# Attention outputs of two heads in the column halves of TensorE's array, and probabilities divided ahead of their transposes

## The reference

```python
def one_block(args):
    blk, qn, qr = args
    s = (jnp.einsum("bqhd,bkhd->bhqk", qn, k_nope) + jnp.einsum("bqhr,bkr->bhqk", qr, k_rope)) * scale
    q_chunk = (blk * Q_BLOCK + jnp.arange(Q_BLOCK)) // CHUNK
    mask = k_chunk[None, :] <= q_chunk[:, None]
    s = jnp.where(mask[None, None], s, -jnp.inf)
    p = jax.nn.softmax(s, axis=-1).astype(v.dtype)
    return jnp.einsum("bhqk,bkhd->bqhd", p, v)
...
return o.reshape(B, S, MLA_HEADS * V_DIM) @ w_o
```

## Time and profile before

| | us |
|---|---|
| median of three runs | 1141.02 |
| the profiled execution | 1142.03 |
| span of its instructions | 1140.2 |
| TensorE busy | 1116.9 (98%) |
| VectorE busy | 874.8 (77%) |
| ScalarE busy | 753.8 (66%) |
| layer 0's head loop, up to the first part of the next slab | 126.6 to 189.2 |
| layer 1's | 552.6 to 615.2 |

### The profile page before, as it was taken

The page is one execution under the profiler, slowest core; times in us unless marked ns, Lnnn a source line. Parts: engine busy times, 40 slices in busy tenths (PEclk is TensorE's granted clock), DMA queues, the critical chain, the costliest instruction groups (busy, mean ns, idle before and its releaser), DMA issues.

```text
span 1140.2 us, 15735 instructions
## 1 busy us (share of the span) xinstructions
PE 1116.9 (98%) x5566; PEld 946.3 (83%) x5566; DVE 874.8 (77%) x983; ACT 753.8 (66%) x941; POOL 35.1 (3%) x64
## 2 busy tenths in 40 slices
PE   9999999999999999999999999999999999999996
PEld 8888888888888888888888888887778887888885
DVE  6568677765554456468676779999999899999997
ACT  6555656455344345556656456799987898988785
POOL 3001000000000001001001000000000000000000
PEclk9999999999999999999999999999999999999999
DMA  9745533668555354646534647999999999999993
GB/s 324 275 147 185 173 95 104 209 216 311 185 184 185 110 182 141 217 135 189 167 102 133 197 174 275 389 403 408 415 417 372 377 402 411 396 417 405 413 369 140
DMA packets 120555, 294.96 MB, mean 259 GB/s; under 512 B 9007, under 2 KB 33677, under 8 KB 119965
## 3 DMA queue, kind: packets, MB, share of 16 engines
q1 hardware_dynamic: 119072, 288.23, 69.8%
q0 software_dynamic: 960, 5.28, 1.2%
q10 hardware_dynamic: 444, 0.47, 0.1%
HBM read 292.90 MB, written 1.05 MB: 258 GB/s over the span
## 4 chain that ended last, share of the span: by engine, by line
PE 77%; DVE 17%; issue 2%; ACT 2%; DMA 1%; ACTq 0%; SPq 0%; DVEq 0%
PE bank L1720 21%; PE bank L1722 21%; PE bank L1721 21%; DVE w_lo L1495 11%; DVE w_lo_more L1495 3%; PE bank L2134 2%; PE bank L1936 2%; PE bank L2135 2%; PE bank L1956 2%; PE bank L1764 2%; PE bank L1944 1%; DVE hid_buf L1634 1%; PE bank L2117 1%; DMA raw<-in_moe_w_gate 1%; PE bank L1925 1%
## 5 line engine op out<-in xcount | busy, mean ns | idle before, releaser
L1166 DVE TENSOR_TENSOR w_lo<-raw,w_hi 128x1024 fp32r<-128x1024 f32 (+4 forms) x141 | 240.3, 1709 | 140.5 <-ACT w_hi L725 139.8
L725 ACT ACTIVATE w_hi<-raw 128x1024 fp32r<-128x1024 f32 (+5 forms) x141 | 201.5, 1433 | 149.0 <-PE bank L1722 149.0
L1495 DVE TENSOR_TENSOR w_lo<-raw,w_hi 128x1792 fp32r<-128x1792 f32 (+3 forms) x148 | 286.4, 1964 | 10.4 <-ACT w_hi L945 9.9
L945 ACT ACTIVATE w_hi<-raw 128x1792 fp32r<-128x1792 f32 (+3 forms) x148 | 244.1, 1668 | 44.7 <-PE bank L1722 29.9
L1720 PE MATMUL bank<-w_hi,aT_hi 128*128 128x512 f32 (+1 forms) x592 | 235.1, 397 | 1.1 <-DVE w_lo L1288 0.6
L1722 PE MATMUL bank<-w_hi,aT_lo 128*128 128x512 f32 (+1 forms) x592 | 229.8, 388 | 0.0
L1721 PE MATMUL bank<-w_lo,aT_hi 128*128 128x512 f32 (+1 forms) x592 | 229.3, 387 | 0.0
L1722 PEld LDWEIGHTS bank<-w_hi,aT_lo 128*128 128x128 f32 x592 | 111.1, 188 | 22.7
L1720 PEld LDWEIGHTS bank<-w_hi,aT_hi 128*128 128x128 f32 x592 | 111.3, 188 | 22.4 <-DVE w_lo L1288 1.6
L1721 PEld LDWEIGHTS bank<-w_lo,aT_hi 128*128 128x128 f32 x592 | 111.4, 188 | 20.3
L1495 DVE TENSOR_TENSOR w_lo_more<-raw,w_hi_more 128x1792 fp32r<-128x1792 f32 (+3 forms) x50 | 96.7, 1940 | 4.5 <-ACT w_hi_more L945 4.5
(11 more groups left out here) (326 smaller groups left out, 1803.1 us busy)
## 6 DMA issues: line engine op xcount, KB each, us to landing
raw<-in_moe_w_gate SPq DMA_DIRECT2D x128, 448.0 KB, 6.6
raw<-in_moe_w_up SPq DMA_DIRECT2D x128, 448.0 KB, 6.4
raw<-in_moe_w_down SPq DMA_DIRECT2D x112, 512.0 KB, 6.6
raw<-in_w_in SPq DMA_DIRECT2D x40, 768.0 KB, 4.4
raw<-in_dense_w_gate SPq DMA_DIRECT2D x22, 512.0 KB, 3.9
raw<-in_dense_w_up SPq DMA_DIRECT2D x22, 512.0 KB, 4.7
raw<-in_dense_w_down SPq DMA_DIRECT2D x11, 1024.0 KB, 4.9
raw<-in_w_in SPq DMA_DIRECT2D x20, 512.0 KB, 4.9
```

The costliest lines, as they stand in the source:

```text
L725: act.activation(dst, src, ACT.Copy).then_inc(hi_made[j], 1)
L945: act.activation(split_of(hi_slot, m), raw_of(i, n), ACT.Copy).then_inc(e_hi_made, 1)
L1166: dve.tensor_tensor(dst, src, high, ALU.subtract).then_inc(lo_made[j], 1)
L1495: dve.tensor_tensor(split_of(lo_slot, m), raw_of(i, n), split_of(hi_slot, m).bitcast(F32), ALU.subtract).then_inc(e_lo_made, 1)
```

## The change

PV is turned around: a head's 64 columns of v are stationary, and pT moves, 256 columns for the first 128 keys and 128 columns for the second (only the second query tile sees those). Two heads make a pair: head x of the pair writes partitions 64x to 64x + 63 of one bank, so its weights stand in one half of the array's columns; the four matmuls alternate between the heads. PV of a pair is issued in even slots from 4 to 18. Its output has channels in the partitions, so VectorE copies it as it is into `oT` (one instruction of 256 columns per pair) and the 16 transposes behind the loop go; ScalarE and VectorE split `oT`, which lies in SBUF, in the places where they split the banks before (`attended_hi`, `attended_lo`).

As tokens are then in the columns, the division by the row sums can't follow PV. VectorE multiplies P by the reciprocals in `p_buf`, ahead of its transposes, and TensorE waits for that (`p_scaled`). VectorE waits for its own reciprocal first. pT has two buffers, for even and odd heads; `qT` has moved to make room. The waits on the count of transposes are renumbered by `transposed`, those on PV by `head_pairs`. Cut to its core:

```diff
-        row_inv = (small[:, 26:28], small[:, 32:34])
+        row_inv = small[:, 26:28]
...
-        mask, p_buf, pT, gain = regions(
-            [("mask", [P, 3 * P]), ("p_buf", [P, 3 * P]), ("pT", [P, 3 * P])],
+        mask, p_buf, pT_even, gain = regions(
+            [("mask", [P, 3 * P]), ("p_buf", [P, 3 * P]), ("pT_even", [P, 3 * P])],
             [("gain", [P, D])])
-        rope_k = place("rope_k", [P, 4, NT, RH])
-        k_rope = place("k_rope", [P, NT, ROPE])
+        rope_k, k_rope, qT = regions(
+            [("rope_k", [P, 4, NT, RH]), ("k_rope", [P, NT, ROPE])],
+            [("qT", [P, S])])
...
-        qT, s_buf = mixed[:, 0, NB:NB + S], mixed[:, 1, NB:NB + 3 * P]
+        s_buf = mixed[:, 1, NB:NB + 3 * P]
+        pT = (pT_even[:, :], mixed[:, 0, NB:NB + 3 * P])
+        oT = xs[:, :, :].rearrange("p t (c s) -> p (t c) s", s=S)
...
+
+        def transposed(use, n):
+
+            return 4 * (use - (use + 2) // 4) + n + 1
+
+        def head_pairs(L, pairs):
+
+            return HEADS // 2 * L + pairs
...
-                pool.wait_ge(o_made, HEADS * (L + 1))
+                pool.wait_ge(o_made, head_pairs(L + 1, 0))
...
                 def transposed_p_in(n):
                     act.wait_ge(p_tr, HEADS * L + n - 1)
-                    if n >= 3:
-                        act.wait_ge(o_made, HEADS * L + n - 2)
-                    act.activation(pT[:, :], bank[B_PT][:, 0:3 * P], ACT.Copy).then_inc(p_in, 1)
+                    if n >= 4:
+                        act.wait_ge(o_made, head_pairs(L, n // 2 - 1))
+                    act.activation(pT[n % 2], bank[B_PT][:, 0:3 * P], ACT.Copy).then_inc(p_in, 1)
+
+                def attended_hi(banks):
+                    act.wait_ge(used[2], B + BLK_GATE + 3)
+                    for n in banks:
+                        act.wait_ge(o_in, head_pairs(L, 2 * n + 2))
+                        act.activation(aT_hi[:, 2 * n:2 * n + 2, :], oT[:, 2 * n:2 * n + 2, :], ACT.Copy).then_inc(tr_hi, 1)
 
                 for n in range(HEADS + 3):
                     if n < HEADS:
...
-                            act.wait_ge(inv_made, HEADS * L + n - 1)
...
                     if n == HEADS + 2:
-                        transposed_hi(4 * L + 1, aT_hi, (0, 1))
+                        attended_hi((0, 1))
...
                 hi(B + BLK_CONV1, 2, SLAB_SIZES[2], B)
-                transposed_hi(4 * L + 1, aT_hi, (2, 3))
+                attended_hi((2, 3))
...
+            def attended_lo(use, banks):
+                for n in banks:
+                    dve.wait_ge(tr_hi, 4 * use + n + 1)
+                    dve.tensor_tensor(aT_lo[:, 2 * n:2 * n + 2, :], oT[:, 2 * n:2 * n + 2, :],
+                                      aT_hi[:, 2 * n:2 * n + 2, :].bitcast(F32), ALU.subtract).then_inc(tr_lo, 1)
...
                 for n in range(HEADS + 3):
                     if 2 <= n <= HEADS + 1:
                         dve.wait_ge(p_made, 2 * (HEADS * L + n - 1))
-                        if n >= 4:
-                            dve.wait_ge(o_in, 2 * (HEADS * L + n - 3))
-                        dve.reciprocal(row_inv[n % 2], row_sum).then_inc(inv_made, 1)
+                        link(dve.reciprocal(row_inv, row_sum))
+                        dve.tensor_scalar(p_buf[:, 0:P], p_buf[:, 0:P], row_inv[:, 0:1], None, ALU.mult).then_inc(p_scaled, 1)
+                        dve.tensor_scalar(p_buf[:, P:3 * P], p_buf[:, P:3 * P], row_inv[:, 1:2], None, ALU.mult).then_inc(p_scaled, 1)
                     if 1 <= n <= HEADS:
                         dve.wait_ge(s_made, HEADS * L + n)
                         if n >= 2:
...
-                    if n >= 3:
-                        dve.wait_ge(o_made, HEADS * L + n - 2)
-                        dve.wait_ge(inv_made, HEADS * L + n - 2)
-                        for t in range(NT):
-                            dve.tensor_scalar(xs[:, t, (n - 3) * VD:(n - 2) * VD], bank[B_O][:, t * VD:(t + 1) * VD],
-                                              row_inv[(n - 1) % 2][:, t:t + 1], None, ALU.mult).then_inc(o_in, 1)
+                    if n >= 4 and n % 2 == 0:
+                        dve.wait_ge(o_made, head_pairs(L, n // 2 - 1))
+                        dve.tensor_copy(oT[:, n // 2 - 2, :], bank[B_O][:, 0:S]).then_inc(o_in, 1)
                     if n == HEADS + 2:
-                        transposed_lo(4 * L + 1, aT_lo, aT_hi, (0, 1))
+                        attended_lo(4 * L + 1, (0, 1))
...
-                transposed_lo(4 * L + 1, aT_lo, aT_hi, (2, 3))
+                attended_lo(4 * L + 1, (2, 3))
...
                     if 2 <= n <= HEADS + 1:
-                        pe.wait_ge(p_made, 2 * (HEADS * L + n - 1))
+                        pe.wait_ge(p_scaled, 2 * (HEADS * L + n - 1))
                         if n >= 3:
                             pe.wait_ge(p_in, HEADS * L + n - 2)
                         for m in range(3):
                             last = pe.transpose(bank[B_PT][:, m * P:(m + 1) * P], p_buf[:, m * P:(m + 1) * P], ident[:, :])
                         last.then_inc(p_tr, 1)
-                    if n == HEADS + 2:
+                    if n >= 4 and n % 2 == 0:
+                        j = n // 2 - 2
+                        pe.wait_ge(p_in, HEADS * L + n - 2)
+                        pe.wait_ge(o_in, head_pairs(L, j))
+                        for kt, keys_part, cols_of in ((0, slice(0, S), slice(0, S)), (1, slice(S, 3 * P), slice(P, S))):
+                            for x in range(2):
+                                last = pe.matmul(bank[B_O][x * VD:(x + 1) * VD, cols_of], v[:, kt, (2 * j + x) * VD:(2 * j + x + 1) * VD],
+                                                 pT[x][:, keys_part], start=kt == 0, stop=kt == 1, skip_group_check=True)
+                        last.then_inc(o_made, 1)
+
+                def half(src, u, sem_ready, value):
+                    def transposes():
                         pe.wait_ge(q_in, HEADS * (L + 1))
                         pe.wait_ge(max_made, 2 * HEADS * (L + 1))
-                        pe.wait_ge(o_in, 2 * (HEADS * L + HEADS // 2))
-                        transpose_tokens(lambda t: xs[:, t, :], tr_made, (0,))
-                    if n >= 3:
-                        pe.wait_ge(p_in, HEADS * L + n - 2)
-                        if n >= 4:
-                            pe.wait_ge(o_in, 2 * (HEADS * L + n - 3))
-                        for t, (m, kt, start, stop) in zip((0, 1, 1), ((0, 0, True, True), (1, 0, True, False), (2, 1, False, True))):
-                            last = pe.matmul(bank[B_O][:, t * VD:(t + 1) * VD], pT[:, m * P:(m + 1) * P],
-                                             v[:, kt, (n - 3) * VD:(n - 2) * VD], start=start, stop=stop)
-                        last.then_inc(o_made, 1)
-
-                def half(src, u, sem_ready, value):
-                    def transposes():
+                        pe.wait_ge(o_in, head_pairs(L + 1, 0))
                         pe.wait_ge(sem_ready, value)
                         transpose_tokens(src, tr_made, (u,))
                     return transposes
 
 
-                slab(L, BLK_CONV1, PAIR_CONV1, bT_hi, bT_lo, None, half(lambda t: xs[:, t, :], 1, o_in, 2 * HEADS * (L + 1)))
+                slab(L, BLK_CONV1, PAIR_CONV1, bT_hi, bT_lo)
```

More of the change, by code:

```diff
@@ L352, in build_trunk @@
             "heads_ready", "keys_moved", "keys_in", "q_tr", "q_in", "s_made", "max_made", "p_made", "p_tr", "p_in", "o_made", "o_in"))
-        inv_made, gate_made, m_made = (sem(n) for n in ("inv_made", "gate_made", "m_made"))
+        p_scaled, gate_made, m_made = (sem(n) for n in ("p_scaled", "gate_made", "m_made"))
         gu_made, silu_made, hid_made, hid_tr, hT_hi_made, hT_lo_made, h_new = (sem(n) for n in (
@@ L738, in transposed_hi @@
                 for n in banks:
-                    act.wait_ge(tr_made, 4 * use + n + 1)
+                    act.wait_ge(tr_made, transposed(use, n))
                     act.activation(dst[:, 2 * n:2 * n + 2, :], bank[B_T + n][:, :].rearrange("p (c s) -> p c s", s=S),
@@ L930, in residual_copies @@
                 for n in banks:
-                    act.wait_ge(tr_made, 28 + n + 1)
+                    act.wait_ge(tr_made, transposed(7, n))
                     act.activation(hT[:, 2 * n:2 * n + 2, :], bank[B_T + n][:, :].rearrange("p (c s) -> p c s", s=S),
@@ L1487, in mixer @@
                     weigh(1)
-                    dve.wait_ge(tr_made, 32)
+                    dve.wait_ge(tr_made, transposed(7, 3))
                     dve.tensor_copy(hT[:, 6:8, :], bank[B_T + 3][:, :].rearrange("p (c s) -> p c s", s=S)).then_inc(hT_dve, 1)
@@ L1945, in mixer @@
                         last.then_inc(p_tr, 1)
-                    if n == HEADS + 2:
-                        pe.wait_ge(q_in, HEADS * (L + 1))
-                        pe.wait_ge(max_made, 2 * HEADS * (L + 1))
-                        pe.wait_ge(o_in, 2 * (HEADS * L + HEADS // 2))
```

(16 more changed lines are left out.)

## The result

The changed kernel takes 1145.22 us (median of 7 runs, 1144.90 to 1145.66), the kernel before, in runs on the same chip, 1141.57 (7 runs, 1140.82 to 1142.12): 1.0031 times as long [1.0022 to 1.0040], 3.65 us more. The forecast was 1148.2 with a range from 1140 to 1157: the sign is right, the size is half of what was forecast (+3.65 against +7.2). The profiled execution took 1144.9, its span is 1143.2.

The account below looks back on a forecast made before the run. TensorE's stream was taken to bound the kernel. Per layer -1.75 (transposes) - 3.8 (PV) + 2.2 (shape changes) + 6.2 (waits) + 0.8 (last PV) = +3.6, twice +7.2 us, giving 1148.2 us, range 1140 to 1157.

Parts of the forecast that it names:

- The bound: Head loop: TensorE's instructions one after the other are the time, busy 62.48 of 62.6 us.
- The waits: TensorE's P transposes wait for the division in even slots 2, 4, 8, 10, 14, 16: 6.2 us a layer.
- none in odd slots: Sign in the waits: TensorE's load waits some 6 us a layer in six even slots, never in odd ones.
- The 16 transposes: Output transposes removed from TensorE's stream, 0.11 each: 1.75 us a layer saved.
- Shape changes: Going into the array's halves and out around each pair's PV: 0.27 us, eight times a layer, 2.2.
- PV of a pair: Two heads' PV in the halves, partly overlapped: 0.88 us a pair, saving 3.8 us a layer.
- the forecast's own sign of being wrong: Wrong if multiplications are far under 0.55, a pair's PV over 1.2 or under 0.7, or TensorE waits behind the loop.
- The last PV: Slot 18, end of the loop: PV waits for ScalarE's copy after the last P transposes, 0.8 us late.
- The head loop: From its first query transposes to the next slab's first product: about 4.5 us longer.
- Serial halves: Rival: a pair's halves run one after the other, PV 1.31 us a pair, total 1155.1 us; chance 0.22.
- Parallel halves without a drain: Rival: PV 0.66 us a pair with no shape-change price, total 1140.2 us, not slower; chance 0.15.
- the waits would not come: Rival: the division's path stays hidden, all of the TensorE saving is kept, 1134.2 us; chance 0.08.

Follow-up runs that it names:

- e1: The changed kernel without the reciprocal and the two multiplications of P: layer 0's head loop 61.01 us instead of 64.85; whole time not comparable.
- e3: The changed kernel with a pair's four matmuls ordered head 0, head 0, head 1, head 1: 1145.47 us, 1.0034 times the kernel before.
- e5: The changed kernel with 128 stationary columns of v, the array's full shape, one head finished before the next: 1153.52 us, 1.0103 times the kernel before.
- e2: The changed kernel with 128 stationary columns of v, the two heads by turns in column regions of one bank: outputs wrong, loop 68.66 us.
- e7: The changed kernel with the division in two parts, the first block's reciprocal and multiplication after the first exponential: 1145.80 us, 1.0036 times the kernel before.

## Why the prediction was right and wrong

- **The bound** was read rightly: TensorE's stream sets the time, no wait of another kind took over, and nothing behind the loop waited (the split of the outputs and the next weights stay hidden).
- **The waits**, the step that set the sign: 6.2 forecast, 6.1 measured, slot by slot as in the table. The share pushed into slots 7 and 13 was named in the working (without a size), while "none in odd slots" among the signs denied it. e1 showed that they are two things on top of each other: 3.9 come with the division, and the 2.2 left under them (2.4 less the 0.2 of slot 2 that was there before) come with PV's move, which brings TensorE to the even slots' transposes before ScalarE's exponentials and copy are done. The forecast had neither that copy nor this split.
- **The 16 transposes**: 1.75 forecast; no run takes them away alone, but the measured sum below closes with it.
- **Shape changes**: 0.27 a pair forecast from 64-row transposes, 0.29 measured at 64 columns (0.09 in, 0.20 out).
- **PV of a pair: the step that failed, as a mis-sized term.** The forecast had "The order is A A B B for the 256 columns and again for the 128, and starts keep their order", which gave 0.88. The trace has 0.70, both heads side by side from 0.01 after the start, and e3 the same with all of one head's matmuls ahead. The halves each take their own matmuls as they come, so 0.66, the lower bound, was nearly the value. I took the middle since no row was near the lower end; the same rows held nothing for the order either. Eight pairs a layer: 8 x 0.18 = 1.4, 2.9 in two layers, of the 3.55 by which the forecast's +7.2 was too high. The 0.70 lies at the edge of the forecast's own sign of being wrong (a pair under 0.7).
- **The last PV**: 0.65, not 0.8.
- **The head loop**: 2.8 longer (62.05 to 64.85), where about 4.5 was forecast; PV of the pairs is 1.4 of the difference.

With the measured terms a layer is -1.75 - 10.9 + 8 x 0.99 + 6.1 + 0.65 = +2.0; the trace has +1.98. Two layers make +4.0, the medians +3.65.

**The rivals.** Serial halves fell: the trace has 0.70 a pair and not 1.31, and e5, which does run one head after the other (without the price of the halves), takes 1153.52. Parallel halves without a drain was half right: parallel they are, but with 0.29 around them a pair costs 0.99, above the 0.71 from which the change would not have been slower. (The Trainium skill, TensorEngine Tiling (Array Packing), Tiling Modes, has both: tiles operate independently, and changing the mode drains the engine; this trace shows 0.01 between the heads' starts for the one and 0.29 for the other.) That the waits would not come fell with the first row of the waits.

## What to carry to other kernels

When work that used to follow a product is moved ahead of it, lay TensorE's path and the other engines' path to that point beside each other slot by slot. The difference is the wait, and the filler work (here the gate chunks) can be moved to where it is missing: +3.65 us became -2.2 with a table of seven numbers and one copy put elsewhere. And when a stage is made cheaper or moved, ask for each slot it leaves whether it was the cover of something else.

## What I had not expected of the hardware

- The column halves of the array take their matmuls independently of the order in the program: a head whose matmuls all stand behind the other's starts 0.02 behind it (e3), with the same total of 0.70 for a pair as by turns.
- They aren't free to enter and leave: 0.29 a visit in this kernel, against none for 128 columns (e5). Two pairs a visit, with four buffers of pT, might halve what the visits cost, an estimate from that number; it wasn't tried.
- A start flag for one column region of a bank took away a neighbouring region's open accumulation in the same partitions (e2, against e5, where only the order differs), while two heads in the same columns and different partitions did not disturb each other (the changed kernel). (The Trainium skill, PSUM — Partial Sum Buffer, The four PSUM rules: a first matmul marks as unwritten its whole bank in the partition quadrants that it writes. What e2 and the changed kernel put out agrees.)
- A reciprocal of one column takes 0.16 us on VectorE, as long as one of two (e7): at this size splitting the reciprocal doubles its time.
